# A state-space scan whose per-head products are done four heads at a time

## The reference, cut to what matters

```python
cum = jnp.cumsum(dtc * A, axis=1)
decay = jnp.exp(jnp.where(causal, cum[:, :, None] - cum[:, None, :], -jnp.inf))
cb = jnp.einsum('btgn,bsgn->btsg', cc, bc)                  # one score block per group
y = jnp.einsum('btsgk,bsgkp->btgkp', cb[..., None] * decay * dtc[:, None], xc)
y = y + jnp.einsum('btgn,bgkpn->btgkp', cc, state) * jnp.exp(cum)[..., None]
state = (state * jnp.exp(cum[:, -1])[..., None, None]
         + jnp.einsum('bsgk,bsgkp,bsgn->bgkpn', jnp.exp(cum[:, -1:] - cum) * dtc, xc, bc))
```

## Time and profile before

| | |
|---|---|
| Median of the runs | 1252.51 us |
| Profiled execution | 1252.64 us, span of the program 1250.7 us |
| TensorE busy / weight loads / DVE / ScalarE / GpSimd | 99% / 88% / 73% / 55% / 6% |
| Granted TensorE clock, mean | 0.999 of full speed |
| The scan's steps | from about 667 to 768 us |

### The profile page before, as it was taken

One profiled execution on the slowest core, in us unless ns is written; L12 is line 12 of the kernel. 1 busy time (PEld: TensorE's weight loads), 2 busy tenths in 40 slices (PEclk: granted clock), 3 DMA queues, 4 the chain that ended last, 5 costly groups with the idle time before them and its releaser, 6 DMA issues.

```text
span 1250.7 us, 18296 instructions
## 1 busy us (share of the span) xinstructions
PE 1237.3 (99%) x7468; PEld 1099.8 (88%) x7468; DVE 919.0 (73%) x1265; ACT 688.5 (55%) x915; POOL 72.8 (6%) x93
## 2 busy tenths in 40 slices
PE   9999999999999999999999999999999999999997
PEld 8878999989988888889998887888888988888886
DVE  6676857875456666667997887788888868788886
ACT  5654344443553444454777776466665574565562
POOL 2000000100000000000002450000000000000000
PEclk9999999999999999999999999999999999999999
DMA  9664645656535556546556554656554744655551
GB/s 294 218 185 141 193 136 181 221 187 210 177 101 168 184 187 201 184 157 203 170 172 209 184 177 151 219 185 202 178 193 139 233 134 134 203 190 182 201 184 52
DMA packets 162594, 225.84 MB, mean 181 GB/s; under 512 B 7853, under 2 KB 123825, under 8 KB 162384
## 3 DMA queue, kind: packets, MB, share of 16 engines
q1 hardware_dynamic: 159392, 214.58, 53.4%
q0 software_dynamic: 2816, 9.51, 2.2%
q10 hardware_dynamic: 304, 0.59, 0.1%
HBM read 223.58 MB, written 1.08 MB: 180 GB/s over the span
## 4 chain that ended last, share of the span: by engine, by line
PE 92%; DVE 5%; ACT 1%; issue 1%; DMA 1%; DVEq 0%; SPq 0%
PE psum L2216 20%; PE psum L2218 20%; PE psum L2217 20%; PE psum L2250 13%; PE psum L2249 7%; PE psum L2247 2%; DVE arena L1893 2%; DVE wlo L1349 2%; PE psum L2248 1%; PE psum L2843 1%; PE psum L2608 1%; PE psum L2587 1%; PE psum L2333 1%; DMA raw<-in_w_in 1%; PE psum L2842 0%
## 5 line engine op out<-in xcount | busy, mean ns | idle before, releaser
L1349 DVE TENSOR_TENSOR wlo<-raw,whi 128x2048 fp32r<-128x2048 f32 (+3 forms) x185 | 415.9, 2260 | 112.9 <-ACT whi L842 111.6
L842 ACT ACTIVATE whi<-raw 128x2048 fp32r<-128x2048 f32 (+3 forms) x185 | 346.0, 1883 | 16.0 <-DMA raw<-in_w_xkv 5.9
L2250 PE MATMUL psum<-h_both,whi 128*128 128x512 f32 x714 | 254.7, 396 | 0.0
L2249 PE MATMUL psum<-h_both,wlo 128*128 128x256 f32 x714 | 199.4, 279 | 0.3 <-DVE h_both L1403 0.3
L2216 PE MATMUL psum<-h_both,whi 128*128 128x256 f32 x688 | 195.9, 285 | 0.0
L2218 PE MATMUL psum<-h_both,wlo 128*128 128x256 f32 x688 | 194.6, 283 | 0.0
L2217 PE MATMUL psum<-h_both,whi 128*128 128x256 f32 x688 | 194.6, 283 | 0.0
L2216 PE MATMUL psum<-whi,r_hi 128*128 128x512 f32 x446 | 176.8, 396 | 0.0
L2218 PE MATMUL psum<-whi,r_lo 128*128 128x512 f32 x446 | 173.9, 390 | 0.0
L2217 PE MATMUL psum<-wlo,r_hi 128*128 128x512 f32 x446 | 173.6, 389 | 0.0
L2250 PEld LDWEIGHTS psum<-h_both,whi 128*128 128x128 f32 x714 | 134.0, 188 | 27.6
(11 more groups left out here) (351 smaller groups left out, 1795.6 us busy)
## 6 DMA issues: line engine op xcount, KB each, us to landing
raw<-in_ffn_up SPq DMA_DIRECT2D x40, 1024.0 KB, 5.1
raw<-in_w_in SPq DMA_DIRECT2D x31, 1024.0 KB, 5.6
raw<-in_ssd_in_proj SPq DMA_DIRECT2D x22, 1024.0 KB, 5.3
raw<-in_ffn_down SPq DMA_DIRECT2D x22, 1024.0 KB, 4.8
raw<-in_w_up SPq DMA_DIRECT2D x16, 1024.0 KB, 5.4
raw<-in_w_down SPq DMA_DIRECT2D x16, 1024.0 KB, 5.0
raw<-in_w_xkv SPq DMA_DIRECT2D x8, 1024.0 KB, 5.1
raw<-in_ssd_out_proj SPq DMA_DIRECT2D x8, 1024.0 KB, 5.0
```

The source lines that it names most:

```text
L842: A(whi[u % SLOTS][:, 0:kt * n], raw[u % SLOTS][:, 0:kt * n], ACT.Copy).then_inc(hi_split, 1)
L1349: V.tensor_tensor(wlo[s][:, 0:kt * n], raw[s][:, 0:kt * n], whi[s][:, 0:kt * n].bitcast(F32), ALU.subtract).then_inc(lo_split, 1)
L2249: M(b[:, 0:T], w_lo_k, h_hi[:, k, :], start=False, stop=False)
L2250: return M(b[:, :], w_hi_k, h_both[:, :, k, :], start=False, stop=k == kt - 1)
```

## The change

TensorE's products of heads 4g to 4g + 3 are all done at head 4g + 5, behind the off-diagonal product of group g + 1, which moves there from head 4g + 4. Heads 28 and 29 are done at head 31, heads 30 and 31 at the tail as before. There are eight decay tables in place of six. Rows are fetched four at a time, at the heads with h % 4 = 1. The score block of an odd group is made at head 8q + 1, three or more steps sooner. ScalarE's and DVE's tables of heads 0 and 1 move to the steps of heads 0 and 1. On DVE `scale_off` moves to head 4g + 2 and the pair of `scale_to_end` to head 8q + 6.

```diff
@@ -65,7 +65,7 @@
 FFN_GROUPS = FFN // 256
 SSD_UNITS, SSD_PER_UNIT = 16, 4
 RESIDUAL_FROM = 2
-SSD_RING = 6
+SSD_RING = 8
 LEAD, LEAD_K = 2 * 256 + SSD_HEADS, (3, 3, 2)
 BC_ORDER = (6, 7, 0, 1, 2, 3, 4, 5)
 
@@ -91,10 +91,13 @@
 
 def scores_after(n):
 
-    what, h = SSD_STEPS[n + 1] if n + 1 < len(SSD_STEPS) else ("none", 0)
+    what, h = SSD_STEPS[n]
     if n == 1:
         return 0
-    return h // 4 if what == "head" and h and h % 4 == 0 else None
+    if what == "head" and h % 8 == 1:
+        return h // 4 + 1
+    what, h = SSD_STEPS[n + 1] if n + 1 < len(SSD_STEPS) else ("none", 0)
+    return h // 4 if what == "head" and h and h % 8 == 0 else None
 
 
 def group_order(groups):
@@ -520,7 +523,7 @@
         negcum = sb("negcum", [P, NT, 2, SSD_HEADS])
         expa = sb("expa", [P, SSD_HEADS])
         crow = sb("crow", [SSD_HEADS, T])
-        dec0 = sb("dec0", [P, TRI])
+        dec0, dec1 = sb("dec0", [P, TRI]), sb("dec1", [P, T])
         decay_rows = nc.dram_tensor("decay_rows", (SSD_HEADS, T), F32, kind="Internal").ap()
         ARENA = 15500
         arena = sb("arena", [P, ARENA])
@@ -577,7 +580,7 @@
         scv = [room(13340 + 512 * b, 2, T) for b in range(2)]
         sxT = [room(14364 + 512 * b, 2, T) for b in range(2)]
         yN = [room(12288 + 1024 * b, NT, MIX) for b in range(2)]
-        dec = [rows[:, 1, T * b:T * b + T] for b in range(4)] + [room(14336 + T * b, T) for b in range(2)]
+        dec = [rows[:, 1, T * b:T * b + T] for b in range(4)] + [room(14336 + T * b, T) for b in range(2)] + [room(15232, T), dec1[:, :]]
         after = dec0[:, 0:P]
         x_end = [dec0[:, 0:T], room(14848, T)]
         cbT = [dec0[:, T:TRI], room(15104, P)]
@@ -691,10 +694,10 @@
                     sp.wait_ge(ssd_y, h - SSD_RING + 1)
                 sp.dma_start(dec[h % SSD_RING], decay_rows[h, :].partition_broadcast(P)).then_inc(row_landed[h % SSD_RING], 16)
 
-            rows_at = {at[("zz", 0, 0)] + SLOTS - 1: [0, 1, 2, 3], at[("zz", 0, 1)] + SLOTS: [4, 5]}
+            rows_at = {at[("zz", 0, 0)] + SLOTS - 1: [0, 1, 2, 3], at[("zz", 0, 1)] + SLOTS: [4, 5, 6, 7]}
             for n, (what, h) in enumerate(SSD_STEPS):
-                if what == "head" and 2 <= h < SSD_HEADS - SSD_RING + 2:
-                    rows_at.setdefault(at[("zz", 0, 0)] + SLOTS + n // SSD_PER_UNIT, []).append(h + SSD_RING - 2)
+                if what == "head" and h % 4 == 1 and 1 < h < SSD_HEADS - 3:
+                    rows_at[at[("zz", 0, 0)] + SLOTS + n // SSD_PER_UNIT] = range(h + 3, h + 7)
             for u, (src, kt, n) in enumerate(units):
                 for h in rows_at.get(u, ()):
                     decay_row(h)
@@ -1148,8 +1151,6 @@
                 for n, (what, h) in enumerate(SSD_STEPS[SSD_PER_UNIT * u:SSD_PER_UNIT * (u + 1)]):
                     if (u, n) == (0, 0):
                         copy_scores(0)
-                        decay(0)
-                        decay(1)
                     if n == 1:
                         if u in (2, 4, 6, 8):
                             for t in range(NT):
@@ -1163,8 +1164,7 @@
                     if what == "head":
                         if h and h % 4 == 0:
                             copy_scores(h // 4)
-                        if h > 1:
-                            decay(h)
+                        decay(h)
                         if h > 8 and h % 8 == 4:
                             group_norm(h // 8 - 1)
                     if what == "tail":
@@ -1978,10 +1978,6 @@
                 for n, (what, h) in enumerate(SSD_STEPS[SSD_PER_UNIT * u:SSD_PER_UNIT * (u + 1)]):
                     if what == "tail":
                         lo_half(1)
-                    if (u, n) == (0, 3):
-                        weigh_decay(0)
-                        scale_off(0)
-                        weigh_decay(1)
                     if n == 3 and u < last_norm:
                         lo_half(0)
                     if n == 1 and 0 < u < last_norm:
@@ -1997,16 +1993,15 @@
                         if h > 8 and h % 8 == 2:
                             add_sums(2 * q - 1)
                             gate(q - 1)
-                        if h > 1:
-                            weigh_decay(h)
-                        if h % 4 == 1 and h > 1:
+                        weigh_decay(h)
+                        if h % 4 == 2:
                             scale_off(h // 4)
                         if h == 1:
                             scale_to_end(1)
-                        if h % 8 == 5 and q < 3:
-                            for g in (2 * q + 2, 2 * q + 3):
-                                scale_to_end(g)
                         if h % 8 == 6:
+                            if q < 3:
+                                for g in (2 * q + 2, 2 * q + 3):
+                                    scale_to_end(g)
                             add_sums(2 * q)
                         if h % 8 == 7 and q < 3:
                             prepare(q + 1)
@@ -2812,7 +2807,7 @@
             xs_transpose(6)
 
 
-            y_bank, y_next, so_banks = [], [], []
+            so_banks = []
 
             def ssd_scores(g):
 
@@ -2824,8 +2819,7 @@
 
                 pe.wait_ge(cb_copied, g + 1)
                 pe.wait_ge(x_end_ready, g + 1)
-                y_next[:] = [claim(("y", g))]
-                M(y_next[0][:, T:2 * T], cbT[g % 2], x_end[g % 2], start=True, stop=True).then_inc(off_done, 1)
+                M(claim(("y", g))[:, T:2 * T], cbT[g % 2], x_end[g % 2], start=True, stop=True).then_inc(off_done, 1)
 
             def ssd_y_of(h):
 
@@ -2835,9 +2829,9 @@
                     for j in range(2):
                         wait_drained(pe, ("xsN", 2 * (h // 8) + j))
                 if h % 4 == 0:
-                    y_bank[:] = y_next
                     pe.wait_ge(off_scaled, h // 4 + 1)
-                y_0, y_1 = [y_bank[0][:, T * t + SSD_P * (h % 4):T * t + SSD_P * (h % 4) + SSD_P] for t in range(NT)]
+                y_bank = bank[use[("y", h // 4)][0]]
+                y_0, y_1 = [y_bank[:, T * t + SSD_P * (h % 4):T * t + SSD_P * (h % 4) + SSD_P] for t in range(NT)]
                 s = dec[h % SSD_RING]
                 M(y_0, s[:, 0:P], xsN[:, 0, xs], start=False, stop=True, skip_group_check=True)
                 M(y_1, s[:, P:T], xsN[:, 1, xs], start=False, stop=True, skip_group_check=True).then_inc(ssd_y, 1)
@@ -2845,10 +2839,13 @@
             def ssd_step(n):
                 what, h = SSD_STEPS[n]
                 if what == "head":
-                    if h >= 2:
-                        ssd_y_of(h - 2)
-                    if h == 1 or h and h % 4 == 0:
+                    if h % 4 == 1:
                         ssd_off(h // 4)
+                        for i in range(max(h - 5, 0), h - 1):
+                            ssd_y_of(i)
+                    if h == SSD_HEADS - 1:
+                        ssd_y_of(SSD_HEADS - 4)
+                        ssd_y_of(SSD_HEADS - 3)
                 if what == "tail":
                     ssd_y_of(SSD_HEADS - 2)
                     ssd_y_of(SSD_HEADS - 1)
```

## The result

The changed kernel takes 1255.77 us (median of 9 runs, 1254.95 to 1257.2), the one before 1252.51 us (9 runs, 1252.16 to 1253.76): ratio 1.0027, 95% interval 1.0018 to 1.0036, so 3.3 us slower. The profiled execution took 1255.78 us, with a span of 1254.0 us against 1250.7.

The account below looks back on a forecast made before the run. TensorE, busy 99% of the span, was taken to bound the kernel; 0.44 + 1.69 + 1.41 at the transposes, + 0.33 at the end, - 0.5 for joins gave +3.4 us: 1255.9 us, range 1252.2 to 1259.0.

Parts of the forecast that it names:

- The joins: Heads joined into shared visits on TensorE: 22 joins save 0.66 us at most, nothing at least; taken as -0.5 us.
- (b): Rival: weight loads inside joint visits overlap better, passes under 0.08 us; 1250.1 us, 1249 with waits low; chance 0.06.
- (d): Rival: a joined head is dearer by one load of 0.11 us that no wide pass hides; 1258.8 us; chance 0.03.
- yT(0): TensorE's transposes at step 19: would wait 0.37 us for ScalarE's group_norm, 0.44 with the late start, at worst 1.16.
- yT(2): TensorE's transposes at step 31: would wait 1.62 us for group_norm, 1.69 with the late start; DVE's shift taken as 0.
- rival (a): The normalisation keeps up: powers come earlier with TensorE, DVE finds idle time for its 1.00 us; 1252.3 to 1254.4; chance 0.29.
- yT(4): TensorE's transposes at step 43: would wait 1.34 us, 1.41 with the late start, with DVE's mean delayed by 1.00 us.
- DVE's 1.00 us: On DVE, scale_off and both scale_to_end, 1.00 us together, move behind r_lo and delay the group's mean by that much.
- the rows by four: Four row fetches in a row: 32 fetches as before, no weight load standing longer behind them; costed at nothing.
- (c): Rival: rows come late and ScalarE holds up its half-splits of the weights; six fetches, 1258.3 to 1262 us; chance 0.08.
- The end: End of the scan: TensorE's 1.43 us wait for DVE's residual grows by 0.33 us, as scale_off(7) comes after r_lo.

## Why the prediction was right, and where not

The forecast, slower by 3.4 us because TensorE gets to the transposes before ScalarE is through, was right in sign, place and sum. Its terms were not all right, and that they add up so well is in part luck.

- **The joins, -0.5 us.** Right: 3.43 + 0.14 + 0.17 us of gaps, less two late starts of 0.06 and 0.07 us that the kernel before had at 685.49 and 740.53 and the changed one has not, plus 0.07 for each of two more visits begun late (five against three), make 3.75; the scan grew by 3.19, so the joins gave about 0.56. Rivals (b) and (d) needed a joint pass under 0.08 us or 0.11 us more a head; a pass took 0.107 and a visit 0.08 less than its parts. The rule behind (d), of the Trainium skill (TensorE: Matmul & The Clock Gate, "Step-by-step: what each phase is for"), describes the load that runs ahead; it does not make a joined head dearer here.
- **yT(0), 0.37 us and 0.07 for the late start.** group_norm ended at 701.63 where 701.65 was worked out; TensorE came at 701.14, not 701.49, and went on 0.05 us after the write, not 0.21 (that handoff was DVE's, this one is ScalarE's). Gap 0.54.
- **yT(2), 1.62 us of cover, and 0 for DVE.** The gap was 1.92, but the step that failed is "ahead of yT(2) I take 0": putting DVE's order back takes away 1.35 us here, and the cover alone leaves 0.57. The term for cover was too large since the power was left where it had stood (722.46); with scale_to_end back it came at 721.65, 0.81 us sooner. To that extent rival (a) was right, that DVE and ScalarE follow TensorE. The two errors nearly cancelled: that 1.69 came near 1.92 is luck.
- **yT(4), 1.34 us, of it 1.00 by DVE.** Measured 0.97; with scale_to_end back there is none, so the 0.34 us left to the cover alone did not come. The handoff was 0.16 us shorter, and the lead was 3.79 us there where 5.40 - 1.84 = 3.56 was taken: the power followed TensorE a little.
- **DVE's 1.00 us as a length that moves.** The moved instructions were costed at 0.42 us each; beside the masks they took up to 1.00. This price was nowhere in the sum. A step costed at nothing, the rows by four, has a part in it: their fetches were indeed never late (no mask is among ScalarE's waits in the scan, so (c) fell as put), but their masks now run four in a row, beside DVE. How large that part is stays open, as one at a time they lengthened a late scale_to_end too.
- **The end, +0.33 us.** 1.60 - 1.43 = 0.17, and 0.14 at heads 28 and 29, where scale_off(7) behind r_lo(5) comes late: 0.31 in two places.

## What to carry to other kernels

Before work is gathered into fewer visits, ask what each visit was covering: take the arrival at the next dependent step less the start of the chain that feeds it, and compare that lead with the chain's length; at yT(2) 0.37 us was to spare, and 1.84 us of work in front was taken away. Put the gathered work in front of the dependent step, not behind it. Count, too, what a burst on one engine does to its neighbours: four transfers fetched together became four masks in a row, which nobody waited for and which made DVE late even on the kernel before. An instruction that is moved beside such work is to be costed at the length that it has there, not at the one in its old place.

## What the runs showed of the hardware

GpSimd's masks and DVE's products with both inputs in SBUF lengthen each other. scale_to_end goes from 0.42 us to between 0.75 and 1.00 in five of eight cases, and back to at most 0.44 with masks of 8 columns. The kernel before has this too, on other products: one of the preparation took 1.23 us in place of 0.68, and a mask 1.82 in place of 0.73. DVE is busy for as long in both (919.0 us before, 918.9 changed, 914.3 with short masks). So the change did not lengthen more of DVE's work in all; the lengthening now falls on the pairs ahead of the mean. The split of the weights in the scan (min/median/max ns), in the changed kernel and then with short masks (the kernel before had up to 1.79 us):

```profile
L1374 DVE TENSOR_TENSOR wlo<-raw,whi x24: 1210/1217/1800, 675.5 to 763.3; 128x1024 fp32r<-128x1024 f32 x24
```

```profile
L1374 DVE TENSOR_TENSOR wlo<-raw,whi x26: 1209/1218/1225, 674.9 to 767.3; 128x1024 fp32r<-128x1024 f32 x26
```

The 32 weighings on DVE, which read one input from PSUM, took 0.40 to 0.42 us in both kernels.

The Trainium skill (SBUF — State Buffer, "Who interferes with whom") states that a DVE instruction with two inputs in SBUF contends with a GpSimd instruction that reads SBUF, that the order of issue decides which one is blocked, and that a DVE instruction with a single SBUF input, outside the 2-port modes, does not contend. The runs agree: the scale_to_end that began at 736.46 inside a run of masks that ended at 737.18 was done at 737.46, and the next one, begun behind it, took 0.41. With scale_to_end late on the kernel before, one that began at 734.08 kept 0.41 us and the mask begun at 734.11 took 0.97; the next, begun at 734.42 inside that mask, took 0.95. In the prediction this rule would have pointed at the moved instructions; their sizes come from the runs.
